# Attention's projections inside the recurrence's preparation, and attention in steps inside the scan

## What is computed

```python
h = rmsnorm(x, mix_pre_g[l])
p = h @ w_in[l]
p_rw, p_diff = p[..., :SHIFT_COLS], p[..., SHIFT_COLS:]
p_rw = p_rw + (token_shift(p_rw) - p_rw) * shift_mu[l]
p_r, p_k, p_v, p_wd, p_ad, p_gd = _split(p_rw, RWKV_COLS)
q_d, k_d, v_d = _split(p_diff, DIFF_COLS)
y_rwkv = rwkv7_group(p_r, p_k, p_v, p_wd, p_ad, p_gd, ...)
y_diff = diff_attention_group(q_d, k_d, v_d, ...)
y = jnp.concatenate([y_rwkv, y_diff], axis=-1) @ w_o[l]
```

## Time and profile before

| | |
|---|---|
| median of three runs | 4218.51 us |
| profiled execution | 4218.56 us |
| its span | 4216.2 us |
| TensorE busy | 3505.6 us, 83% |
| TensorE weight loads | 2668.2 us, 63% |
| VectorE busy | 1771.0 us, 42% |
| ScalarE busy | 1208.1 us, 29% |
| GpSimd busy | 144.2 us, 3% |
| mean granted TensorE clock | 0.879 |
| moved by DMA | 285.23 MB, 68 GB/s |

### The profile page before, as it was taken

How to read it: one execution, slowest core, us unless ns; L and a number is a source line. 1 busy time by engine, 2 the same in 40 slices (tenths; PEclk the granted TensorE clock), 3 DMA queues, 4 the chain that set the end, 5 groups by cost and what they waited for, 6 DMA issues and landing times. The chain is left out here.

```text
span 4216.2 us, 43446 instructions
## 1 busy us (share of the span) xinstructions
PE 3505.6 (83%) x17694; PEld 2668.2 (63%) x17694; DVE 1771.0 (42%) x2710; ACT 1208.1 (29%) x1738; POOL 144.2 (3%) x174
## 2 busy tenths in 40 slices
PE   8999954987999859668886699976987789689986
PEld 6887832775688747544344588745765677467764
DVE  4456454333544535624643333233642323443323
ACT  3333224113433222132222222232344211232322
POOL 0000000110000000000000000000002420000000
PEclk9999976766999979878998899987988987899998
DMA  3244300000333512110001122311220000122222
GB/s 129 97 150 151 104 25 8 2 2 18 98 100 120 195 63 82 65 50 15 0 25 65 50 95 95 95 55 50 89 77 21 22 16 21 60 66 90 85 85 70
DMA packets 75220, 285.23 MB, mean 68 GB/s; under 512 B 8336, under 2 KB 8464, under 8 KB 73872
## 3 DMA queue, kind: packets, MB, share of 16 engines
q1 hardware_dynamic: 75024, 282.47, 20.2%
HBM read 276.15 MB, written 6.29 MB: 67 GB/s over the span
## 5 line engine op out<-in xcount | busy, mean ns | idle before, releaser
L147 DVE TENSOR_TENSOR wlo<-raw,whi 128x1024 fp32r<-128x1024 f32 x450 | 552.1, 1227 | 1486.6 <-ACT whi L142 1486.4
L142 ACT ACTIVATE whi<-raw 128x1024 fp32r<-128x1024 f32 x450 | 476.3, 1059 | 1567.1 <-PE ps L233 1142.2
L231 PE MATMUL ps<-h_hi,wlo 128*128 128x512 f32 x968 | 389.6, 402 | 94.8 <-DVEq L202 94.8
L232 PE MATMUL ps<-h_lo,whi 128*128 128x512 f32 x968 | 388.0, 401 | 0.0
L233 PE MATMUL ps<-h_hi,whi 128*128 128x512 f32 x968 | 387.6, 400 | 0.0
L169 PE MATMUL ps<-h_hi,wlo 128*128 128x512 f32 x832 | 341.4, 410 | 41.0 <-PEq L78 21.2
L171 PE MATMUL ps<-h_hi,whi 128*128 128x512 f32 x832 | 328.4, 395 | 0.0
L170 PE MATMUL ps<-h_lo,whi 128*128 128x512 f32 x832 | 328.4, 395 | 0.0
L231 PEld LDWEIGHTS ps<-h_hi,wlo 128*128 128x128 f32 x968 | 185.5, 192 | 144.3 <-issue 99.2
L169 PEld LDWEIGHTS ps<-h_hi,wlo 128*128 128x128 f32 x832 | 158.6, 191 | 89.0 <-issue 41.2
L233 PEld LDWEIGHTS ps<-h_hi,whi 128*128 128x128 f32 x968 | 185.2, 191 | 45.5
(11 more groups left out here) (516 smaller groups left out, 6023.6 us busy)
## 6 DMA issues: line engine op xcount, KB each, us to landing
raw<-in_wstream SPq DMA_DIRECT2D x453, 512.0 KB, 3.4
mod_ring<-in_wmod SPq DMA_DIRECT2D x48, 512.0 KB, 4.5
c_rows<-in_c_rows SPq DMA_DIRECT2D x3, 1024.0 KB, 5.6
x<-in_x_t SPq DMA_DIRECT2D x4, 512.0 KB, 8.6
x_saved<-x SPq DMA_DIRECT2D x1, 2048.0 KB, 11.1
x<-x_saved SPq DMA_DIRECT2D x1, 2048.0 KB, 7.8
mix_saved_d<-x SPq DMA_DIRECT2D x1, 2048.0 KB, 8.1
mix_back<-mix_saved_d SPq DMA_DIRECT2D x1, 2048.0 KB, 8.3
```

The costliest lines, as they stand in the source:

```text
L142: act.activation(k.whi[:, n % SPLIT, :], k.raw[:, n % RAW, :], ACT.Copy).then_inc(k.hi_ready, 1)
L147: dve.tensor_tensor(k.wlo[:, n % SPLIT, :], k.raw[:, n % RAW, :], k.whi[:, n % SPLIT, :].bitcast(F32), ALU.subtract).then_inc(k.split_read ...
L231: pe.matmul(out, lo, xhi, start=first, stop=False)
L232: pe.matmul(out, hi, xlo, start=False, stop=False)
```

## The change

**Projections.** `Shifted` keeps the 15 chunks of the recurrence (`SHIFTED = 15`). The other 12 become a `Background` of 96 slices, in banks 6 and 7, which `rwkv_prepare` deals out as 12, 24, 24, 9, 9, 9 and 9.

**Preparation.** One stage in place of the load stage, three stages, a set of turns and the bonus product: v is turned first, `lora` is loaded by its first instruction, all logarithms stand ahead of all exponentials, and each group ends with bonus times v. `g_up` is loaded in a stage of its own right ahead of the scan.

**Matrices and inversions.** They stay alone. `rwkv_matrices` has two banks for its products (three before) and one for both results of a job; `invert` uses four banks in place of six.

**Attention.** `attention_prepare` turns v and computes lambda. The 16 jobs become 34 steps of `DiffAttention`, one, two and two in the three gaps of each scan step until they are used up. An even step holds the turns of the job before, then the scores of this one (banks 4, 5), the masking and the maximum, and the exponentials; an odd one the reciprocals and the combination, and the output product in bank 7. Scores are no longer issued ahead. The norm of attention's output comes after `rwkv_finish`.

**Products without use.** `keep_busy` issues 128x128 products of two constant matrices into bank 1: 20 at the scan's start, 3 ahead of each of two waits of a step.

**Places.** All buffers of the mixer have fixed places in one arena. The products and sums of attention and recurrence themselves are the same as before.

```diff
-        k.chunk += 27
+        k.chunk += SHIFTED
...
+            if i:
...
                 self.dve_mix(dve, i - 1)
+        self.dve_mix(dve, SHIFTED - 1)
...
+class DiffAttention:
...
+    JOBS = [(h, i) for h in range(4) for i in range(TT)]
+    STEPS = 2 * len(JOBS) + 2
...
+        for step in gap:
+            n = step // 2
+            if step % 2 == 0:
+                if n:
+                    h, i = jobs[n - 1]
+                    pe.wait_ge(self.p_ready, n)
+                    if n >= 2:
+                        pe.wait_ge(self.pt_ready, n - 1)
+                    for j in range(i + 1):
+                        mm = pe.transpose(k.ps[:, 6, j * P:(j + 1) * P],
+                                          self.s[:, 2 * ((n - 1) % 2), j * P:(j + 1) * P], mat(k, "ident"))
+                    mm.then_inc(self.turned, 1)
+                if n < len(jobs):
+                    h, i = jobs[n]
+                    w = (i + 1) * P
+                    if n:
+                        pe.wait_ge(self.masked, 2 * n)
+                    for c in range(2):
+                        r = slice(64 * c, 64 * c + 64)
+                        mm = pe.matmul(k.ps[:, 4 + c, 0:w], self.q[r, h, i * P:(i + 1) * P], self.kk[r, h, 0:w],
+                                       start=True, stop=True)
+                    mm.then_inc(self.scores_ready, 1)
+            elif n and jobs[n - 1][1] == TT - 1:
+                h = jobs[n - 1][0]
+                pe.wait_ge(self.pt_ready, n)
+                if h:
+                    pe.wait_ge(self.out_used, h)
+                for j in range(TT):
+                    mm = pe.matmul(k.ps[:, 7, j * P:512], self.vt[:, j, h * P:(h + 1) * P],
+                                   self.pt[:, j, j * P:512], start=j == 0, stop=j == TT - 1)
+                mm.then_inc(self.out_ready, 1)
...
+            w = (self.JOBS[n][1] + 1) * P
+            if step % 2 == 0:
+                dve.wait_ge(self.scores_ready, n + 1)
+                if n >= 2:
+                    dve.wait_ge(self.turned, n - 1)
+                for c in range(2):
+                    e = 2 * (n % 2) + c
+                    if w > P:
+                        dve.tensor_copy(s[:, e, 0:w - P], k.ps[:, 4 + c, 0:w - P])
+                    dve.tensor_tensor(s[:, e, w - P:w], k.ps[:, 4 + c, w - P:w], mat(k, "after"),
...
+            else:
+                e = 2 * (n % 2)
+                for c in range(2):
+                    dve.wait_ge(self.exp_ready, 2 * n + c + 1)
+                    dve.reciprocal(st[:, e + c, 3:4], st[:, e + c, 2:3]).then_inc(self.rec_ready, 1)
...
+def rwkv_prepare(k, rw, v_tok, sig, iclr, kk, sq, th, lora, pc, w65, i65, p65, q65, one65, lora_d, bg):
...
+    gaps = bg.gaps(12, 24, 24, 9, 9, 9, 9)
...
+            bg.pe(pe, gaps[0])
+            pe.wait_ge(loaded, 16)
+            pe.wait_ge(tanh_ready, 1)
+            pe.wait_ge(v_kept, TT)
+            for n in range(8):
+                c, x, o = n % 4, th if n < 4 else wa, slice(0, 64) if n < 4 else slice(64, 128)
...
+            bg.pe(pe, gaps[1])
+            for c in range(4):
+                pe.wait_ge(sq_ready, c + 1)
+                pe.wait_ge(sig_ready, 3 + c)
+                pe.matmul(k.ps[:, sum_bank(c), :], mat(k, "ones64"), sq[:, c, :], start=True, stop=True)\
+                  .then_inc(sum_ready, 1)
+            bg.pe(pe, gaps[2])
+            pe.wait_ge(sig_ready, 8)
+            for c in range(4):
+                pe.wait_ge(rk_ready, c + 1)
+                if c >= 2:
+                    pe.wait_ge(clamped, c - 1)
+                pe.matmul(k.ps[:, c, :], mat(k, "ones64"), sq[:, c, :], start=True, stop=True).then_inc(bonus, 1)
+                bg.pe(pe, gaps[3 + c])
...
+            bg.act(act, gaps[1])
+            for c in range(4):
+                act.wait_ge(clamped, c + 1)
+                act.activation(sq[:, c, :], sq[:, c, :], ACT.Ln, scale=float(2 ** 30)).then_inc(log_ready, 1)
+            for c in range(4):
+                act.wait_ge(log_ready, c + 1)
+                act.activation(sq[:, c, :], sq[:, c, :], ACT.Exp, scale=-0.5, bias=k.eps["two15"])\
+                   .then_inc(inv_ready, 1)
+            bg.act(act, gaps[2])
...
+            bg.dve(dve, gaps[2])
+            for c in range(4):
+                dve.wait_ge(inv_ready, c + 1)
+                dve.tensor_tensor(kk[:, c, :], kk[:, c, :], sq[:, c, :], ALU.mult).then_inc(kk_done, 1)
...
+                dve.wait_ge(bonus, c + 1)
+                dve.tensor_tensor(v[:, c, :], v[:, c, :], k.ps[:, c, :], ALU.mult).then_inc(done, 1)
+                bg.dve(dve, gaps[3 + c])
...
-            ps, hp, tk = k.ps[:, n % 3, :], slice(64 * q, 64 * q + 64), slice(T * P, T * P + P)
-            if n >= 3:
-                pe.wait_ge(arb_ready, 2 * (n - 2))
+            ps, hp, tk = k.ps[:, n % 2, :], slice(64 * q, 64 * q + 64), slice(T * P, T * P + P)
+            if n >= 2:
+                pe.wait_ge(arb_ready, 2 * (n - 1))
...
+        def keep_busy(pe, n):
+
+            for _ in range(n):
+                pe.matmul(k.ps[:, 1, 0:P], mat(k, "ident"), mat(k, "ones"), start=True, stop=True)
...
+            keep_busy(pe, 20)
...
                 mm.then_inc(as_ready, 1)
+                bg.pe(pe, gaps[3 * j])
+                keep_busy(pe, 3)
                 pe.wait_ge(r0_ready, j + 1)
                 for h in range(8):
-                    mm = pe.matmul(k.ps[tp, 1, h * 64:h * 64 + 64], xt[tp, h, T, :], r0[tp, h * 64:h * 64 + 64],
+                    mm = pe.matmul(k.ps[tp, 0, h * 64:h * 64 + 64], xt[tp, h, T, :], r0[tp, h * 64:h * 64 + 64],
                                    start=True, stop=True)
                 mm.then_inc(u_done, 1)
+                bg.pe(pe, gaps[3 * j + 1])
+                keep_busy(pe, 3)
                 pe.wait_ge(u_ready, j + 1)
...
                 dve.tensor_tensor(r0[tp, :], k.ps[tp, 0, :], rv[tp, T, :], ALU.add).then_inc(r0_ready, 1)
+                bg.dve(dve, gaps[3 * j])
+                bg.dve(dve, gaps[3 * j + 1])
                 dve.wait_ge(s_done, j + 1)
...
+                bg.dve(dve, gaps[3 * j + 2])
                 dve.wait_ge(y_done, j + 1)
...
+def mixer(k, rw, qkv, yd, bg, rs, lora_d, g_up_d):
...
+    rwkv_prepare(k, rw, v_tok, sig, b_t, a_t, sq, th, lora, pc, w65, i65, p65, q65, one65, lora_d, bg)
...
+    attention_prepare(k, v_d, vt, lam)
...
+        diff = DiffAttention(k, ctx, q, kk_d, vt, yd, s, pt, st, lam[:, 5:6])
+        for c in range(4):
+            rwkv_matrices(k, c, rw, a_t, b_t, v_tok, tri, arb, rv, y, Idle(), (0, 0))
+            invert(k, [tri[:, g, :] for g in range(2)],
+                   [xt[:, 2 * c + g, :, :].rearrange("p a n -> p (a n)") for g in range(2)], tmp)
...
+        transpose_tiles(k, [(b_t, b_tok), (rw[:, 7:11, :], k_tok)])
+        g_up = at(k, "g_up", 14, [P, 2, 512])
+        with stage(nc, "loaded") as (block, loaded):
+            @block.sync
+            def _(sp):
+                sp.dma_start(g_up[:, :, :], g_up_d.rearrange("p (a n) -> p a n", a=2)).then_inc(loaded, 16)
+                sp.wait_ge(loaded, 16)
+        rwkv_scan(k, rw, a_t, pc, v_tok, b_tok, k_tok, xt, arb, rv, y, at(k, "state", 102, [P, 2, 4, P]),
+                  at(k, "r0", 106, [P, 512]), at(k, "u", 108, [P, 512]), at(k, "sum", 18, [P, 4, 64]),
...
+                  diff, (1, 2, 2))
...
+        def dve_evac(dve, i, bg):
+            dve.wait_ge(k.chunk_done, bg.g0 + i + 1)
+            dve.tensor_tensor(qkv[:, i, :], bg.bank(i), rs, ALU.mult).then_inc(bg.left, 1)
+        bg = Background(k, ctx, 12, hm, (6, 7), nothing, dve_evac, 192)
```

More of the change, by code:

```diff
@@ L866, in invert @@
         eye = k.mats[:, MAT["eye"], 0:64]
[L867 removed]
+        tx, out = [k.ps[:, g, 0:256] for g in range(2)], [k.ps[:, 2 + g, 0:256] for g in range(2)]
         blocks = [(slice(64 * b, 64 * b + 64), slice(64 * p, 64 * p + 64)) for p in range(4) for b in range(2)]
@@ new lines, in gaps, with sp, pe @@
+    def gaps(self, *counts):
+        out = []
+        for c in counts:
+            end = min(self.STEPS, self.at + c)
+            out.append(range(self.at, end))
+            self.at = end
+        return out
+    def sp(self, sp, gaps):
+        pass
+    def pe(self, pe, gap):
+        k, jobs = self.k, self.JOBS
+        for step in gap:
[29 more added lines that the diff above has]
+                mm.then_inc(self.out_ready, 1)
@@ L1522, in at @@
+    rwkv_finish(k, rw, y, g_up, four("mean", 78), four("sq_y", 86))
+    norm_tiles(k, [yd[:, h, :] for h in range(4)], lambda h: lam[:, 6:7], 1.0 / P, 1e-5,
+               place=(four("sq_d", 54), four("lg_d", 62), four("rs_d", 70)))
 def at(k, name, kb, shape, dtype=F32):
```

596 lines of the change are left out of this document (249 added, 347 removed).

## The result

The changed kernel took 4144.06 us, median of four runs (4141.8 to 4147.4), against 4218.71 for the kernel before beside it (4218.38 to 4219.48): a ratio of 0.9823, 95% interval 0.9806 to 0.984, 74.7 us less. The forecast was 4147 us, 4100 to 4188. The profiled execution took 4143.16 us with a span of 4141.3 and a mean granted clock of 0.893 (0.879 before).

What follows compares the result with a forecast made beforehand. Stages stand in a row, so each one's idle time is on the path; VectorE bounds the new scan. The touched stretch's terms sum to an end at 959.6 against 1031.2 us, 71.6 less: 4147 us, range 4100 to 4188.

Steps and rivals of the forecast that it cites:

- 7.13 + 0.6 + 1.91: Preparation: VectorE's time per channel group, old work plus bonus times v plus a chunk's split and evacuation, taken as 9.7 us.
- a quarter of the rounds' difference: Matrices and inversions: four rounds, 175.6 us before, taken as 172.6 by one quarter of one slow-to-quick round's difference.
- the two lengths named: Matrices and inversions: a round is still either 36 or 46 us.
- fewer banks cost nothing: Matrices: two product banks instead of three and one for two results, priced at zero.
- the waits for exponentials: Scan with attention: VectorE's waits for exponentials, 15.6 us in 16 jobs before; ten jobs keep theirs, 9.8 us.
- The waits for scores: Scan with attention: VectorE waits for turns and scores; nine waits remain, 12.2 us at full clock or 20.3 at half.
- ends and rest: Scan's sum: filler start 6.1 or 11.9 us, last updates 7.8 or 16.5, output products 2.7 or 12.5, late state products.
- later state products: Scan, within ends and rest: state products late at half clock, 0 us at full or 14.6 at half.
- The bounds of the scan: Scan with attention: VectorE's queue summed to 116.5 us at full clock, 163.5 at half; about 0.75 taken, 140 us.
- Rivals 1 and 2: Scan: full clock, 116.5 us, kernel 4123, chance 0.25; or half clock, 163.5 us, kernel 4171, chance 0.22.
- slices whose splits come late: Preparation, rival 4: VectorE and TensorE alternate, stage 115 to 130 us, kernel 4165 to 4180; chance 0.07.
- stay at half through the slices: Preparation onward, rival 3: half clock through slices, matrices and scan, preparation 161 us, kernel 4255, slower; chance 0.04.

Runs made afterwards that it cites:

- the three runs: Changed kernel with none, 136 (as it stands) and 272 records of products without use in the scan: 4146.12, 4144.06 and 4146.07 us.

## Why the prediction was right

By its own steps, predicted and measured us in the profiled execution:

| step | predicted | measured |
|---|---|---|
| projections' stage ends at | 488.3 | 488.0 |
| preparation with slices | 97.5 | 99.2 |
| turns of v, lambda | 4.8 | 4.9 |
| four rounds of matrices | 172.6 | 165.5 |
| turns of b and k | 5.5 | 5.2 |
| wait for g_up | 4.3 | 3.6 |
| scan with attention | 140 | 140.4 |
| finish, norm | 46.6 | 46.2 |
| stretch ends at | 959.6 | 953.0 |
| the rest of 4147 or 4143.16 | 3187.4 | 3190.2 |

The stretch was shortened by what the prediction named, and the runs with each overlap undone show it. That the total came within 4 us has luck in it: the rounds of matrices came 7.1 us under the sum, and the rest of the kernel, which differs by more than that between kernels with the same code there, 2.8 over. The working's small slips (7.13 + 0.6 + 1.91 is 9.6 and not 9.7, the last group 11.6 and not 11.9, a quarter of the rounds' difference 2.9 and not 3.0) come to less than 1 us.

**The preparation** went as its queue said: a clock of 0.95, one wait of 5.18 us on TensorE where some 5 were named, and VectorE bound behind it with 9.47 us for two of its groups (9.7 predicted) and 10.70 for the first. TensorE's later waits are 2.0, 2.2 and 0.6 us, a little under the 2.7. The run with the slices apart shows that the cover is real, at 29 us.

**The matrices** came out 7.1 us under: two rounds were quick, and I had spread one quarter of one round's difference. The rounds were 46.3, 37.1, 35.7 and 46.4, of the two lengths named. Which of them is quick was luck in the forecast, and it changes even between kernels with the same code ahead (last section). That fewer banks cost nothing, as priced, holds: at 1.00 a round's products took 14.3 us before and after.

**The scan** agrees in its sum to 0.4 us, and less well in its parts. VectorE's own and attention's work was 77.9 in the sum and 77.7 in the trace (there with the two memsets, 1.0 us), the waits for exponentials 9.8 and 9.3. The waits for scores were under-sized: 12.2 to 20.3 in the sum, 24.9 measured, in 12 waits of 2.1 us where nine were counted. Their reason was the one given (scores behind the turns, as the run with scores first shows). What made up for it was the other side: "ends and rest" adds up to 16.6 us at full and 55.5 at half clock, some 37 at 0.74 by a straight line, and the trace has 62.7 - 24.9 - 9.3 = 28.5. The start's wait of 7.2 us lay in its 6.1 to 11.9, but for later state products, which half clock was to make dearer by 14.6 us, VectorE waited only 3.2. VectorE's idle time was 62.7 us, just over the 35 to 60 named.

**The clock's price was too high.** The bounds of the scan were 116.5 us at full clock and 163.5 at half, 9.4 us for each tenth of clock. From the first sum on, the runs took 133.8 us at 0.60, 130.9 at 0.74 and 125.4 at 0.87, so 3.1 us for each tenth. The filler's own time in the queue is in that slope, so the clock's price by itself isn't shown. At 0.60, near attention's 0.62, the stage took 138.2 us without filler, some 143 with the changed kernel's start, and not 150 to 160. Rivals 1 and 2 did not occur: the scan with attention reached neither 1.00 nor 0.50 in any run (0.60 to 0.87). A straight line through the three runs would put such a scan, with the same start, at some 132 and 148 us and not at 116.5 and 163.5; that is an estimate. Since the stage took 138.2, 140.4 and 139.5 us at three clocks so far apart, 140 from the middle of two bounds that are both doubtful was partly luck. The prediction's own statement, that VectorE is the bound and TensorE's work fits beside it, should have made the bounds narrow.

Of the other rivals, slices whose splits come late did not appear: TensorE waited for the bonus sums' input (10.0 us in four waits) and not for a split. The clock did not stay at half through the slices either (0.95).

The rule of the Trainium skill (TensorE: Matmul & The Clock Gate, "What's actually happening") that the clock follows how busy TensorE has been was set aside in the prediction because of the old scan's row. The traces do not agree with it for these small products: by the profile's busy time TensorE was busy for 20.3 of 20.3 us at 0.50 in a round of matrices, while another round with the same products kept 1.00. The measurement decides here.

## What to carry to other kernels

When two chains share an engine's queue, sum that queue first. Here its busy time (77.9 us summed, 77.7 measured) and its waits for exponentials (9.8 and 9.3) came out right; the waits for the other engine at a changed clock did not, so give those a narrow price only when a run has shown it. A clock or filler of an engine that isn't the bound moves the stage only by what is on the way to the bound. Within one step, issue what waits for the older result ahead of what waits for the newest one; that exchange of two blocks was worth 11 us here. And before a gain is put down to an overlap, run the cheap part of the change alone: the filler by itself gave the old kernel 24 us, and in the new one nothing that could be measured.

## What the hardware showed that was not expected

- Matrices' products are the same in each round, and TensorE hardly waits in them; at 1.00 eight jobs take 14.3 us, and 25.7 where they are at 0.50 throughout (first round of the kernel before). No round that fell to 0.50 left it before the inversion, and in the run with 16 full-size products of filler a round the first stayed at 0.50 for 32 us. In the inversion the clock rose, in the first round of the changed kernel at 625.3 us, 7 us after the inversion's first product.
- With the filler in the inversions, quick and slow rounds alternate: 35.2, 46.0, 36.3, 46.2 us in one kernel and 46.4, 35.1, 46.1, 35.4 in another, with the same code up to the rounds. Where the rounds start does not decide it by itself: at 594.12 us in the first of these and at 594.15 in the second. From the first product of the rounds to the last it is 162 to 167 us in every kernel but two (174.7 with the filler in the matrices, 174.8 in the kernel before). What decides which round is quick stays open.
- The old scan's ring holds 1.00 with six 128x128 products a step and 20 at its start, and has 0.52 without. In the matrices, where TensorE hardly waits, such products left the first round at 0.50.
